# Ten stages of a transformer kernel read their split activations from other start bytes in SBUF

## The reference, cut to what matters

```
for l in range(DEPTH_2):
    h = rms_norm_2(x, ffn1_norms[l, 0])
    x = x + 0.5 * rms_norm_2(swiglu(h, ffn1_w13[l], ffn1_w2[l]), ffn1_norms[l, 1])
    h = rms_norm_2(x, mix_norms[l, 0])
    y = token_mixing(h, w_in[l], ...)
    x = x + rms_norm_2(y, mix_norms[l, 1])
    h = rms_norm_2(x, cross_norms[l, 0])
    m = rms_norm_2(mem, cross_norms[l, 2])
    x = x + rms_norm_2(cross_attention_2(h, m, ...), cross_norms[l, 1])
    h = rms_norm_2(x, ffn2_norms[l, 0])
    x = x + 0.5 * rms_norm_2(swiglu(h, ffn2_w13[l], ffn2_w2[l]), ffn2_norms[l, 1])
```

## Time and profile before

| | us |
|---|---|
| median of three runs | 2031.33 (2027.0 to 2035.44) |
| the profiled execution | 2027.11 |
| its span, first to last instruction | 2024.8 |
| TensorE matmuls busy | 1988.5 (98%) |
| weight loads busy | 1836.8 (91%) |
| VectorE busy | 1344.6 (66%) |
| ScalarE busy | 1084.5 (54%) |

### The profile page before, as it was taken

How to read it: one execution, slowest core, us unless ns; L and a number is a source line. 1 busy time by engine, 2 the same in 40 slices (tenths; PEclk the granted TensorE clock), 3 DMA queues, 4 the chain that set the end, 5 groups by cost and what they waited for, 6 DMA issues and landing times.

```text
span 2024.8 us, 36880 instructions
## 1 busy us (share of the span) xinstructions
PE 1988.5 (98%) x14968; PEld 1836.8 (91%) x14968; DVE 1344.6 (66%) x1876; ACT 1084.5 (54%) x1708; POOL 49.9 (2%) x47
## 2 busy tenths in 40 slices
PE   7999999999999999999999999999999999999998
PEld 7989988999899989899998998999899989887887
DVE  6786866777566667866777554655477668756554
ACT  5855555554454454556466444644454565646443
POOL 0021000000000000000100000000000001000000
PEclk9999999999999999999999999999999999999999
DMA  7522454655566557534553655565555535545553
GB/s 271 168 85 75 154 182 159 205 198 188 176 218 192 198 166 231 184 134 136 198 198 136 219 187 189 195 208 190 197 199 186 176 115 177 177 165 177 180 187 124
DMA packets 98726, 359.25 MB, mean 177 GB/s; under 512 B 11192, under 2 KB 11512, under 8 KB 98296
## 3 DMA queue, kind: packets, MB, share of 16 engines
q1 hardware_dynamic: 98560, 356.90, 52.0%
HBM read 353.65 MB, written 1.05 MB: 175 GB/s over the span
## 4 chain that ended last, share of the span: by engine, by line
PE 90%; DVE 5%; ACT 3%; issue 1%; DMA 0%; SPq 0%; DVEq 0%; ACTq 0%
PE ps L1031 15%; PE ps L1033 14%; PE ps L1032 14%; PE ps L1018 7%; PE ps L1105 7%; PE ps L1107 7%; PE ps L1106 7%; PE ps L1218 2%; PE ps L1220 2%; PE ps L1219 2%; PE ps L1187 2%; PE ps L1073 2%; PE ps L1074 2%; PE ps L1072 2%; PE ps L1188 2%; PE ps L1194 2%
## 5 line engine op out<-in xcount | busy, mean ns | idle before, releaser
L1717 DVE TENSOR_TENSOR wlo<-raw,whi 128x1024 fp32r<-128x1024 f32 x635 | 774.3, 1228 | 449.3 <-ACT whi L2451 447.2
L2451 ACT ACTIVATE whi<-raw 128x1024 fp32r<-128x1024 f32 x635 | 665.9, 1056 | 372.9 <-PE ps L1107 153.9
L1031 PE MATMUL ps<-H,whi 128*128 128x256 f32 x2288 | 645.4, 282 | 1.3 <-DVE wlo L1717 1.3
L1033 PE MATMUL ps<-H,wlo 128*128 128x256 f32 x2288 | 636.6, 278 | 0.0
L1032 PE MATMUL ps<-L,whi 128*128 128x256 f32 x2288 | 636.3, 278 | 0.0
L1031 PEld LDWEIGHTS ps<-H,whi 128*128 128x128 f32 x2288 | 429.3, 188 | 6.8 <-issue 3.5
L1032 PEld LDWEIGHTS ps<-L,whi 128*128 128x128 f32 x2288 | 429.2, 188 | 0.6
L1033 PEld LDWEIGHTS ps<-H,wlo 128*128 128x128 f32 x2288 | 429.6, 188 | 0.0
L1105 PE MATMUL ps<-whi,HH 128*128 128x512 f32 x440 | 171.3, 389 | 0.0
L1107 PE MATMUL ps<-wlo,HH 128*128 128x512 f32 x440 | 171.2, 389 | 0.0
L1106 PE MATMUL ps<-whi,HL 128*128 128x512 f32 x440 | 171.2, 389 | 0.0
(11 more groups left out here) (439 smaller groups left out, 3166.3 us busy)
## 6 DMA issues: line engine op xcount, KB each, us to landing
raw<-in_ws SPq DMA_DIRECT2D x635, 512.0 KB, 3.6
prow<-in_rows SPq DMA_DIRECT2D x11, 512.0 KB, 5.9
row<-in_rows SPq DMA_DIRECT2D x9, 512.0 KB, 6.1
mema<-in_memT SPq DMA_DIRECT2D x4, 512.0 KB, 5.2
mema<-in_mem2T SPq DMA_DIRECT2D x4, 512.0 KB, 6.6
memb<-in_mem2T SPq DMA_DIRECT2D x4, 512.0 KB, 5.7
DT<-in_dec SPq DMA_DIRECT2D x2, 768.0 KB, 6.2
X<-in_x SPq DMA_DIRECT2D x1, 1024.0 KB, 11.1
```

What stands on the lines that cost most here:

```text
L1031: e.matmul(o, h, hs[k], start=first and k == 0, stop=False, skip_group_check=True)
L1033: mm = e.matmul(o, lo, hs[k], start=False, stop=last and end, skip_group_check=True)
L1717: e.tensor_tensor(m.wlo[:, n % SPL, :], r, h.bitcast(F32), SUB).then_inc(*c.lo.done(n))
L2451: e.activation(m.whi[:, n % SPL, :], m.raw[:, n % RAW, :], ACT.Copy).then_inc(*c.hi.done(n))
```

## The change

The table of begins has other numbers for the ten stages whose activation moves. Each stage has the same begin for H and for L, as before. The begins of standing activations stay 0.

```
-BEGIN = {"x0": (64, 64), "mix": (0, 0), "c": (64, 64), "f": (64, 64), ("a", 0): (64, 64), ("m", 0): (64, 64), ("o", 0): (0, 0), ("c", 0): (64, 64), ("b", 0): (64, 64), ("a", 1): (64, 64), ("m", 1): (64, 64), ("o", 1): (0, 0), ("c", 1): (64, 64), ("b", 1): (0, 0)}
+BEGIN = {"x0": (48, 48), "mix": (0, 0), "c": (80, 80), "f": (72, 72), ("a", 0): (48, 48), ("m", 0): (72, 72), ("o", 0): (0, 0), ("c", 0): (56, 56), ("b", 0): (80, 80), ("a", 1): (56, 56), ("m", 1): (48, 48), ("o", 1): (0, 0), ("c", 1): (88, 88), ("b", 1): (0, 0)}
```

## The result

The changed kernel takes 2048.14 us, the median of four runs (2045.4 to 2051.63), against 2033.38 for the kernel before (four runs, 2027.0 to 2037.31). The ratio is 1.007 with a 95% interval of 1.0052 to 1.0087: slower by 14.8 us between the medians, where 16.6 us faster was forecast. The profiled execution took 2051.63 us with a span of 2049.5, 24.7 more than the span before.

The account below looks back on a forecast made before the run. TensorE's matmuls, busy 98% of the span, bound the kernel: their number times their pace. f and b turning quick (9.4 us) plus half the other 3216 (7.2) gave 16.6 us less, 2014.7, say 2015; range 2004 to 2037.

Parts of the forecast that it names:

- Below and beyond these there is no row: H and L matmuls: trace shows no pace outside 113.3 and 117.8 ns; such paces were given little chance.
- The step of 34.8 us beyond: All 7824 H and L matmuls at a third pace one step slower: 34.8 us on top of 11.1; given little.
- two of the rivals that the text did price, 2038 and 2042: Extra 16-byte lines touched, 6.4 us more, chance 0.05; quick stages and short quick stretches falling, 11.1 us more, chance 0.09.
- The begin that all ten stages share serves two of them and fails eight: All stages at 64: only both a quick; others, given new begins, forecast to gain 9.4 (f, b) plus 7.2 us.
- Both a keep their pace: Both layers' a stages, 2112 matmuls: forecast to stay at the quick pace at begins 48 and 56.
- The rival of the falling stages: Both a stages lose their quick pace at 48 and 56, others stay: 9.4 us more, 2042 with short stretches; chance 0.09.
- No lottery in time: H and L streams: pace chosen when a stream begins, held until broken, and chosen alike when the same program returns.
- The count of quick matmuls: Short quick stretches in mixers and x0, counted as 384 matmuls beside the 2112 of the a stages.
- Nothing is given back by the feed: Weights feeding TensorE: they arrive in time at 113.4 ns, so a gained step isn't lost as a wait.
- H standing at 72 and 48: Mixers' rv and dv, 96 matmuls a layer at 233 ns: change taken as 0, at most 1.3 us either way.
- The rule of 16-byte lines: Moving reads starting 8 bytes off a multiple of 16 touch 65 lines, not 64: 6.4 us more, 2038; chance 0.05.
- The independent ports: LDWEIGHTS has a read port independent of the moving operand's, so begins can't make reads disturb each other; speaks for no change.

Follow-up runs that it names:

- the run with ten begins: Kernel before with a different begin for each of the ten stages (f 128, first a 192, first b 96, second a 160, others): 2043.25 us, with 2033.88 before.

## Why the prediction was wrong

- **What bounds the kernel: right.** Instructions and waits are the same, and the pace of the matmuls that move H and L makes 23.7 us between the two profiled executions, whose spans are 24.7 apart.
- **That a begin sets the pace: right in kind.** The rows at 64 and 0 for a standing operand said so, and it is so for moving ones.
- **The step that failed** is "Below and beyond these there is no row", with the little I gave to a further pace. I took the two paces of one begin, 113.3 and 117.8, for the two that the machine has, so a new begin could only give the one or the other. Begins have paces of their own: 120.0 at 0, 116.7 and 117.8 at 32, 118.3 at 48, 118.4 at 56, 121.6 at 72, 120.0 at 80. The step of 34.8 us beyond stood in the text as a bound, and was left out of the range. So were two of the rivals that the text did price, 2038 and 2042; the range ended at 2037.
- **"The begin that all ten stages share serves two of them and fails eight"**, from which I took that another begin would serve the eight: wrong. 117.8, the longer pace of 64, is still better than what any of the five new begins gave in the profiled stages. None of f, b, x0, c and the mixers turned quick, where 16.6 us were forecast from them; they lost 12.9 (4.0, 2.3, 0.7, 0.9, 3.9, 1.1).
- **Both a keep their pace: wrong.** They lost 10.8 us, 5.3 and 5.5. The rival of the falling stages had named 9.4 us for them, and that 48 and 56 give less than the quick pace of 64 was right. It missed that the others could fall as well. And 64 by itself is no promise: with the rest of the changed kernel around them both a stages came out at 117.8.
- **"No lottery in time": half right.** In the large stages the choice at 64 was the same in both profiles of the kernel before and, but for the edited stage, where only the first a was edited. In eight units of x0 it changed from one execution to the other. With other work ahead it went the other way, both in a and in b.
- **The count of quick matmuls: 96 too high.** In each mixer 48 are quick from 915.3 us and 48 from 939.9, not 72 from 912.3 and 72 from 937.0. That makes 288 for 384, or 0.4 us, and changes nothing in the argument.
- **Nothing is given back by the feed: not put to the test by the change**, but by 112. There TensorE waits 2.4 us for wlo at L1031 instead of 1.3, and the median is 15.8 us less all the same.
- **H standing at 72 and 48: right**, 233.3 ns both before and after, in both mixers.
- **The rule of 16-byte lines** (the Trainium skill, "SBUF — State Buffer", Specifications (TRN2)): not what is seen. The begins 48 and 80, multiples of 16, cost 5.0 and 2.2 ns; those 8 bytes off (56, 72, 88, 104, 120) are never under 118.3, but 0, 96 and 128 aren't either, and 8 gave 118.0 in a c stage. Whether a line more costs its share can't be told under effects this large.
- **The independent ports** (the Trainium skill, "SBUF — State Buffer", section "A bandwidth-pool intuition that's wrong"): the run with both operands at 64 speaks against taking it as no influence at all. The moving operand stayed, the standing one moved by 64 bytes, and the pace went to 120.0 everywhere. If the ports are separate, the two reads meet elsewhere.

Settled by runs: the pace goes by the distance between the starts of the moving and the standing operand (0, 64 and 112 each at two places), over a whole stream of three matmuls for each tile. Distances beyond 256 bytes weren't tried.

Argued only: that the kernel before spreads over 13 us (2024.37 to 2037.31) because 64 has two paces and streams choose between them, where 112 has one. No run without a profile shows its paces, and a rival explains the other kernels: the granted clock. The changed kernel spreads over 6.2 us, from 2045.4 at a mean clock of 0.999 to 2051.63 at 0.996, and the one with mha and BRH at 112 over 5.0, from 2008.0 at 0.999 to 2012.99 at 0.996. The kernel before doesn't follow its clock (2024.37 and 2031.0 both at 1.0), which leaves room for the draw of paces.

Open: what in the chip makes the paces, and what picks one of several. Two things in the traces narrow it down. A settled stream repeats a short pattern of distances. With all begins at 128 it is five long in all four stages (122, 120, 119, 115, and 117 or 118 ns), at 96 it is six long (118, 121, 117, 125, 116, 123, in the stage b of the run with ten begins), at 0 it is 120 each time. Five isn't a multiple of the three matmuls of a product, so it isn't one kind of matmul that pays. And a stream can reach its pattern after a start that isn't in it, as the timeline with all begins at 112 shows.

## What to carry to other kernels

When TensorE never waits and matmuls of one shape start at unequal distances in different stages, look at where the two operands begin against one another; a change of some bytes moved the pace of such matmuls by up to 7% here (113.3 to 121.6 ns), and the kernel's time by 0.7 to 1.1%. Try begins in the whole kernel at once and read the pace of each stage, and don't tune them stage by stage: what a begin of several paces gives depends on more than the stage, so look for one that gives the same in all stages. Here that was 112, and 0 and 128 at slower paces. Keep high and low parts at the same begin: the one mix tried, of 112 and 64, was slower than either.

## What the runs showed of the hardware

The paces of 256-column fp32r matmuls in long streams, by begin of the moving operand against weights at a multiple of 512, in ns: 0: 120.0. 16: 116.7, 118.6, 120.1. 32: 116.7, 117.8. 48: 118.3. 56: 118.4. 64: 113.3, 117.8. 72: 121.6. 80: 118.4, 120.0. 96: 119.9. 104: 120.1. 112: 113.3 (114.4 on average where other work breaks the streams). 120: 120.8. 128: 118.6. 160: 118.5. 176: 119.3. 192: 117.7. 240: 117.1. A pace at 48 or 112 is the same in every long stream that was profiled; 16, 32, 64 and 80 gave two or three. For 512 columns it is the other way round, best with both at one place: 226.7 to 226.9 at distance 0 (HH before, H at 0, both at 64), 228.9 with whi 64 beyond HH, 233.3 with H 64, 72 or 112 beyond whi. The granted clock fell to its lower level for 3.4 or 6.8 us at a time, up to four times in an execution and in some not at all; in the profiled execution after, each time soon after TensorE had waited 1.3 to 2.1 us.
